# The state space quarters of a two-block transformer kernel: three elementwise products and a difference placed on GpSimd beside VectorE's scans

## The chip, the cores and the metric

One core of a Trainium2 chip runs the whole program. The metric is the device time of one execution in microseconds (us). All data are float32.

## The reference, cut to what matters

Two blocks run one behind the other on x of shape 1 x 256 x 1024. The first has attention, a pooling mixer and two grouped mixtures of experts; the second a mixer of two halves (mLSTM and a diagonal state space), a feed-forward layer, a gated linear mixer and another feed-forward layer. The change touches only the state space half:

```
ab_re, ab_im = mag * cos(a_im * dt), mag * sin(a_im * dt)
bu_re = einsum('blgp,gnp->blgn', ug, bb_re)
bu_im = einsum('blgp,gnp->blgn', ug, bb_im)
...
_, _, x_re, x_im = lax.associative_scan(_complex_affine_combine, (a_seq_re, a_seq_im, bu_re, bu_im), axis=1)
y = einsum('blgn,gpn->blgp', x_re, c_re) - einsum('blgn,gpn->blgp', x_im, c_im)
y = y + d_skip * ug
```

There are 32 groups of 64 states, 2048 complex states in all, over 256 steps.

## The kernel before, in words

The kernel is a list of stages. In each, TensorE, ScalarE, VectorE and GpSimd run a program of their own, and all wait for each other at the stage's end (`stage_done`, L231 to L237). Weights stream through a ring of six buffers, issued by SyncE. `mixer_ab` (L1877) is one such stage: `all_pe` (L1932), `all_act` (L2071), `all_dve` (L2112), and no program on GpSimd. The output projection behind it is the next stage (`project_out`, L1780, its matmuls at L1789), and the feed-forward layer follows.

The 2048 states are worked in four quarters of 512 (four columns of 128 partitions, 256 steps each), so an array of one quarter is 128 x 1024. The complex recurrence is made real: the input is turned back by the angle of the step, the two parts are scanned with the real decay `mag`, and the result is turned forward. `cosT` and `sinT` hold the tables. For quarter c:

- `states(c)` (TensorE, L1944) puts the real and imaginary inputs in PSUM and signals `bu_ready`.
- `turn_in` (VectorE, L2118, products at L2127): four products of a PSUM operand and a table, into z0, z1, t_re, t_im; the last signals `bu_taken`.
- `turned_in` (L2131): z0 += t_re (L2133), z1 -= t_im (L2134).
- `scans` (L2136): eight scans of 128 x 256, real and imaginary by turns (L2139, L2140), from z0 to t_re and z1 to t_im. The decay is one column repeated.
- `turn_out` (L2143): z0 = t_re cos (L2146), z1 = t_im cos (L2147), t_re *= sin (L2148), t_im *= -sin (L2149); the last signals `x_ready`.
- `outputs(c)` (TensorE, L1954, matmuls at L1960) waits for `x_ready` and signals `y_ready`; `take_y` (L2151, L2153) adds the skip term.

The tiles z0, z1 lie in the ring buffer's scratch, t_re in `xn`, t_im in `gates`, the tables in `arena`: all in SBUF. The trace uses these names.

The mLSTM half is interleaved by hand. VectorE's order (L2265 to L2312): quarter 0; four convolutions (L2158, L2161), each waiting for its projection tile, which ScalarE takes from PSUM (L2074); `take_y(0)`; quarter 1; `forget`; `take_y(1)`; `log_forget`; quarter 2 with `sums` (L2183, waits for TensorE's running sums, L2038 to L2040) between its scans and `turn_out`; `running_max`; `take_y(2)`; quarter 3 with the attention-like pieces between its parts: `floor`, `weigh(h)` (L2202, one SBUF and one PSUM operand) and `finish(h)` (L2210 to L2215: small ops on 128 x 2, two of them with two SBUF operands, then two of 128 x 128 from PSUM); then the norms and the gates.

TensorE's order (L1994 to L2069): projections to the state space with `states(0)` and `states(1)` among them; `outputs(0)`; the q, k, v blocks and `states(2)`; the gate products (48 matmuls of 8 columns, L2025); `outputs(1)`; the Z projections (L1941, 64 matmuls, `states(3)` among them); the running sums; `outputs(2)`; scores and mixes by head; `outputs(3)`.

Of the kernel before, what the change touches and what calls it, by code (L numbers as in the profile page):

```python
# [13 lines left out]
ALU = mybir.AluOpType  # L14
# [139 lines left out]
def build_program(nc, A, out):  # L154

    with ExitStack() as ctx:
# [3 lines left out]
        def sem(name):  # L160
            return ctx.enter_context(nc.semaphore(name))
# [20 lines left out]
        col_at, n = {}, 0  # L182
# [38 lines left out]
        chain = {}  # L221
# [87 lines left out]
        cosT, sinT = take(S_PAIRS, S), take(S_PAIRS, S)  # L309
# [254 lines left out]
        x_ready, h_act, h_dve = sem("x_ready"), sem("h_act"), sem("h_dve")  # L564
# [1312 lines left out]
        def mixer_ab():  # L1877
# [6 lines left out]
            for c in range(2):  # L1884
# [11 lines left out]
            t1, t2, t3, b_tok, a_tok, m_tok = (take(TT, 4) for _ in range(6))  # L1896
# [5 lines left out]
            a_rows, m_rows = scratch[:, 5632:5888], scratch[:, 5888:6144]  # L1902
            z = scratch[:, 6144:8192].rearrange("p (a q s) -> p a q s", a=2, q=4)
# [9 lines left out]
            den = small[:, 36:52].rearrange("p (h t b) -> p h t b", h=4, t=2)  # L1913
            var_ready, sd_ready = head_norm_signals
            exp_ready, ln_ready = log_sigmoid_signals
            (tile_ready, tile_taken, spread_ready, conv_ready, conv_done, abs_ready, lf_ready, b_ready, a_ready, aT_ready,
             m_ready, mT_ready, em_ready, qk_ready, ex_ready, w_ready, num_ready, num_taken, hn_ready, hnT_ready) = (
                sem("ab_" + n) for n in (
                    "tile_ready", "tile_taken", "spread_ready", "conv_ready", "conv_done", "abs_ready", "lf_ready", "b_ready",
                    "a_ready", "aT_ready", "m_ready", "mT_ready", "em_ready", "qk_ready", "ex_ready", "w_ready", "num_ready",  # L1920
                    "num_taken", "hn_ready", "hnT_ready"))
            bu_ready, bu_taken, x_ready, y_ready, y_taken, g_done, glu_ready, sig_ready = (
                sem("s5_" + n) for n in ("bu_ready", "bu_taken", "x_ready", "y_ready", "y_taken", "gelu_done", "glu_ready",
                                         "glu_sig_ready"))
            US, XM, QKV, VT, GATES, Z = 0, 4, 8, 20, 22, 23
            QK, LG, NUM, GLU, Y = (4, 0), (5, 1), (6, 2), (3, 7, 0, 1), 7

# [4 lines left out]
            def all_pe(pe):  # L1932
# [19 lines left out]
                    ins.then_inc(bu_ready, 1)  # L1952

                def outputs(c):  # L1954
                    pe.wait_ge(x_ready, c + 1)
                    if c:
                        pe.wait_ge(y_taken, c)
                    for i, (n, part) in enumerate(((0, z[:, 0]), (1, z[:, 1]), (1, t_re), (0, t_im))):
                        for q in range(4):
                            ins = pe.matmul(ps[32 * q:32 * q + 32, Y, 0:S], CT[:, n, c, 32 * q:32 * q + 32], part[:, q, :],  # L1960
                                            start=(i == 0), stop=(i == 3))
                    ins.then_inc(y_ready, 1)
# [71 lines left out]
                release(pe)  # L2034

                pe.wait_ge(tile_taken, Z + 4)
                pe.wait_ge(lf_ready, 1)
                pe.matmul(ps[:, 4, 0:4], const("upto"), t1[:, 0, :], start=True, stop=True)  # L2038
                pe.matmul(ps[:, 4, 4:8], ones, t1[:, 0, :], start=True, stop=False)
                pe.matmul(ps[:, 4, 4:8], const("upto"), t1[:, 1, :], start=False, stop=True).then_inc(b_ready, 1)  # L2040
                pe.wait_ge(a_ready, 1)
# [4 lines left out]
                pe.wait_ge(m_ready, 1)  # L2046
# [5 lines left out]
                for h in range(4):  # L2052
                    if h < 3:
                        scores(h + 1)
                    if h == 0:
                        pe.wait_ge(em_ready, 1)
                    mix(h)
                outputs(3)
                w = ring.take(pe, ("glu",))
# [11 lines left out]
            def all_act(act):  # L2071
# [16 lines left out]
                act.wait_ge(abs_ready, 1)  # L2088
# [5 lines left out]
                for h in range(4):  # L2094
                    act.wait_ge(qk_ready, h + 1)
                    if h >= 2:
                        act.wait_ge(w_ready, h - 1)
                    lg = ps[:, LG[h % 2], :]
                    act.activation(expd[:, h % 2, 0:S], lg[:, 0:S], ACT.Exp, bias=a_tok[:, 0, h:h + 1])
                    act.activation(expd[:, h % 2, S:W], lg[:, S:W], ACT.Exp, bias=a_tok[:, 1, h:h + 1]).then_inc(ex_ready, 1)  # L2100
                    if h == 0:
                        act.wait_ge(em_ready, 1)
# [9 lines left out]
            def all_dve(dve):  # L2112
                v = chain["dve"]
# [15 lines left out]
                        ins.then_inc(bu_taken, 1)  # L2129

                def turned_in(c):  # L2131
                    dve.wait_ge(bu_taken, c + 1)
                    dve.tensor_tensor(z[:, 0], z[:, 0], t_re, ALU.add)  # L2133
                    v(dve.tensor_tensor(z[:, 1], z[:, 1], t_im, ALU.subtract))  # L2134

                def scans(c, pairs):  # L2136
                    for q in pairs:
                        decay = pc[:, 0, 4 * c + q:4 * c + q + 1].to_broadcast([P, S])
                        dve.tensor_tensor_scan(t_re[:, q, :], decay, z[:, 0, q, :], 0.0, ALU.mult, ALU.add)  # L2139
                        ins = dve.tensor_tensor_scan(t_im[:, q, :], decay, z[:, 1, q, :], 0.0, ALU.mult, ALU.add)  # L2140
                    v(ins)

                def turn_out(c):  # L2143

                    co, si = rotation(c)
                    dve.tensor_tensor(z[:, 0], t_re, co, ALU.mult)  # L2146
                    v(dve.tensor_tensor(z[:, 1], t_im, co, ALU.mult))  # L2147
                    dve.tensor_tensor(t_re, t_re, si, ALU.mult)  # L2148
                    dve.scalar_tensor_tensor(out=t_im, in0=t_im, scalar=-1.0, in1=si, op0=ALU.mult, op1=ALU.mult).then_inc(x_ready, 1)  # L2149

                def take_y(c):  # L2151
# [18 lines left out]
                def forget():  # L2170
                    dve.wait_ge(tile_taken, GATES + 1)
                    v(dve.tensor_tensor(pre, pre, b_if.unsqueeze(1).to_broadcast([P, TT, 8]), ALU.add))
                    v(dve.tensor_scalar(t2, f, -1.0, None, ALU.mult))
                    dve.tensor_tensor(t2, f, t2, ALU.min).then_inc(abs_ready, 1)
                    v(dve.tensor_scalar(t1, f, 0.0, None, ALU.min))

                def log_forget():
                    dve.wait_ge(ln_ready, 2)
                    dve.tensor_tensor(t1, t1, t2, ALU.subtract).then_inc(lf_ready, 1)

                def sums():
                    dve.wait_ge(b_ready, 1)
                    v(dve.tensor_copy(b_tok, ps[:, 4, 0:8].rearrange("p (t h) -> p t h", t=TT)))  # L2183
                    dve.tensor_tensor(a_tok, pre[:, :, 0:4], b_tok, ALU.subtract).then_inc(a_ready, 1)

                def running_max():
                    dve.wait_ge(aT_ready, 1)
                    v(dve.tensor_copy(a_rows[0:4, :], ps[0:4, 5, 0:S]))
                    v(dve.tensor_tensor_scan(m_rows[0:4, :], ones[0:4, 0:1].to_broadcast([4, S]), a_rows[0:4, :], 0.0,
                                             ALU.mult, ALU.max))  # L2190
                    dve.tensor_scalar(m_rows[0:4, :], m_rows[0:4, :], -1.0, None, ALU.mult).then_inc(m_ready, 1)

                def floor():
                    dve.wait_ge(mT_ready, 1)
                    dve.tensor_tensor(t1, b_tok, ps[:, 6, 0:2 * P].rearrange("p (t h) -> p t h", t=TT)[:, :, 0:4],
                                      ALU.subtract).then_inc(em_ready, 1)

                def weigh(h):
                    dve.wait_ge(ex_ready, h + 1)
# [65 lines left out]
                for i in range(4):  # L2265
                    turn_in(0, i)
                turned_in(0)
                scans(0, range(4))
                turn_out(0)
                for n in range(4):  # L2270
                    convolve(n)
# [1 line left out]
                for i in range(4):  # L2273
                    turn_in(1, i)
                turned_in(1)
                scans(1, range(4))
                turn_out(1)
                forget()
                take_y(1)
# [1 line left out]
                for i in range(4):  # L2281
                    turn_in(2, i)
                turned_in(2)
                scans(2, range(4))
                sums()
                turn_out(2)
                running_max()
# [4 lines left out]
                        floor()  # L2292
                turned_in(3)
                weigh(0)
                scans(3, range(2))
                weigh(1)
                finish(0)
                scans(3, range(2, 4))
                weigh(2)
                finish(1)  # L2300
                turn_out(3)
# [9 lines left out]
                mlstm_out()  # L2311
                glu_out(3)  # L2312

            stage(all_pe, all_act, all_dve)
            scratch_used = 4 * len(programs["pe"])
            stream.append(lambda sp: sp.wait_ge(stage_done, scratch_used))
            project_out("ab_out", mixT, 0, col("norm_g_2", 16, 8))
# [371 lines left out]
```

## Time and profile before

| | |
|---|---|
| median of 3 runs | 2192.69 us (2184.86 to 2197.79) |
| profiled execution, its own time | 2188.47 us |
| its span, first to last instruction | 2186.4 us |
| busy, TensorE / VectorE / ScalarE / GpSimd | 1731.5 / 501.8 / 218.1 / 97.9 us |
| mean granted TensorE clock | 0.881 of full speed |
| the `mixer_ab` stage's state space part | 1345 to 1454 us of the span |

The profiler calls the engines PE (matmul), PEld (weight load), DVE (VectorE), ACT (ScalarE), POOL (GpSimd) and SP (SyncE). A timeline row gives the start, the duration, the engine and line, the operation, its tiles as output<-inputs, their shapes and the number of instructions merged in the row; in brackets the idle time before it and what ended it. Consecutive VectorE instructions overlap a little in the records, so the distance from start to start is what one costs. Columns of the tables by stretch are explained at their first group below.

### The profile page before, as it was taken

How to read it: one execution, taken by the hardware profiler on the slowest of the kernel's cores; microseconds unless marked ns; L12 is line 12 of the kernel's file. 1: busy time of each engine (PE TensorE's matmuls, PEld its weight loads, DVE VectorE, ACT ScalarE, POOL GpSimd, SP SyncE). 2: the span in 40 equal slices, each digit the busy share in tenths (PEclk: the TensorE clock that was granted, in tenths of full speed). 3: DMA queues.
4: the chain of work that ended last, by engine and by line, in shares of the span. 5: the costliest groups of instructions: out<-in, count | busy, mean ns of one | idle time of the engine just before them, and what ended most of it. 6: DMA issues, size and time to landing. Idle time of an engine off the chain costs nothing. (4 is left out here: it accounts for less than half of the span.)

```text
span 2186.4 us, 22473 instructions
## 1 busy us (share of the span) xinstructions
PE 1731.5 (79%) x9018; PEld 1000.1 (46%) x9019; DVE 501.8 (23%) x1168; ACT 218.1 (10%) x510; POOL 97.9 (4%) x125
## 2 busy tenths in 40 slices
PE   5999978866666576776666657878999899889998
PEld 3755553322222253232222215646885486558853
DVE  1213362111101125411111016861000203420001
ACT  1001020000000020000000001321000212110000
POOL 1010010000000007500000000000000000000000
PEclk9999968978877867898787778889999899899999
DMA  9969249999999956799999994133335434124330
GB/s 363 385 234 406 93 181 402 421 422 422 422 422 422 409 233 250 322 406 421 422 422 422 422 408 158 39 140 122 142 107 210 164 116 154 39 87 154 116 135 19
DMA packets 122665, 581.10 MB, mean 266 GB/s; under 512 B 10820, under 2 KB 15272, under 8 KB 67160
## 3 DMA queue, kind: packets, MB, share of 16 engines
q1 hardware_dynamic: 120416, 573.90, 65.4%
q0 software_dynamic: 1104, 2.86, 0.4%
q10 hardware_dynamic: 1064, 3.17, 0.4%
q8 instruction: 60, 0.98, 0.2%
q14 instruction: 21, 0.17, 0.0%
HBM read 578.86 MB, written 1.05 MB: 265 GB/s over the span
## 5 line engine op out<-in xcount | busy, mean ns | idle before, releaser
L1306 PE MATMUL ps<-ring_buffer,arena 128*32 128x512 f32 x2048 | 309.6, 763 | 170.6 <-DMA ring_buffer<-in_exp_w 167.9
L1831 PE MATMUL ps<-hT,ring_buffer 128*128 128x256 f32 x1408 | 309.9, 382 | 4.1 <-issue 2.6
L1831 PEld LDWEIGHTS ps<-hT,ring_buffer 128*128 128x128 f32 x1408 | 268.7, 192 | 45.2 <-issue 6.3
L1306 PEld LDWEIGHTS ps<-ring_buffer,arena 128*32 128x32 f32 x2048 | 82.1, 135 | 384.8 <-issue 325.0
L1331 PE MATMUL ps<-ring_buffer,arena 128*32 128x512 f32 x1088 | 155.8, 725 | 100.3 <-DMA ring_buffer<-in_exp_w 89.3
L1839 PE MATMUL ps<-ring_buffer,arena 128*128 128x512 f32 x352 | 154.2, 595 | 3.0 <-DVE arena L1872 1.9
L1331 PEld LDWEIGHTS ps<-ring_buffer,arena 128*32 128x32 f32 x1088 | 41.0, 130 | 204.3 <-issue 191.6
L1496 DVE TENSOR_TENSOR arena<-arena,ps 128x512 f32<-128x512 f32 x18 | 19.2, 1065 | 411.6 <-PE ps L1306 411.6
L1839 PEld LDWEIGHTS ps<-ring_buffer,arena 128*128 128x128 f32 x352 | 65.9, 190 | 90.4 <-issue 87.8
L1276 PE MATMUL ps<-arena,xn 128*128 128x128 f32 x640 | 82.0, 289 | 12.9 <-DVE arena L1466 12.9
L1276 PEld LDWEIGHTS ps<-arena,xn 128*128 128x128 f32 x640 | 78.6, 203 | 28.1 <-issue 22.3
L2364 PE MATMUL ps<-hT,ring_buffer 128*128 128x256 f32 x384 | 87.1, 389 | 1.9 <-issue 1.0
L1872 DVE TENSOR_TENSOR arena<-arena,ps 128x256 f32<-128x256 f32 x44 | 18.5, 421 | 295.9 <-ACT arena L1866 295.9
L2364 PEld LDWEIGHTS ps<-hT,ring_buffer 128*128 128x128 f32 x384 | 74.4, 195 | 15.0 <-issue 3.5
L1419 ACT ACTIVATE arena<-ps,mod,gain 128x128 f32<-128x128 f32 x72 | 27.1, 457 | 419.0 <-PE ps L1276 419.0
L1789 PE MATMUL ps<-ring_buffer,hT 128*128 128x512 f32 x128 | 59.7, 627 | 3.3 <-DVEq L237 3.0
L715 PE MATMUL ps<-hT,ring_buffer 128*128 128x256 f32 x256 | 58.6, 391 | 3.2 <-ACTq L237 2.5
L1512 DVE TENSOR_TENSOR arena<-ps,gates 128x512 f32<-128x512 f32 x16 | 11.1, 692 | 211.8 <-PE ps L1331 211.8
L1345 PE MATMUL ps<-arena 128*128 128x512 f32 x128 | 59.3, 605 | 0.0
L499 PE MATMUL ps<-ring_buffer,arena 128*32 128x512 f32 x384 | 50.0, 642 | 9.2 <-DMA ring_buffer<-in_ada_w 8.3
L715 PEld LDWEIGHTS ps<-hT,ring_buffer 128*128 128x128 f32 x256 | 50.0, 197 | 13.0 <-issue 3.4
L1436 ACT ACTIVATE arena<-ps 128x512 f32<-128x512 f32 x18 | 10.8, 597 | 416.7 <-PE ps L1306 416.7
(501 smaller groups left out, 1565.5 us busy)
## 6 DMA issues: line engine op xcount, KB each, us to landing
ring_buffer<-in_exp_w SPq DMA_DIRECT2D x384, 1024.0 KB, 18.6
ring_buffer<-in_ffn_w SPq DMA_DIRECT2D x30, 2048.0 KB, 7.9
ring_buffer<-in_ada_w SPq DMA_DIRECT2D x24, 2048.0 KB, 12.6
ring_buffer<-in_c_w_in SPq DMA_DIRECT2D x8, 2048.0 KB, 7.8
ring_buffer<-in_attn_w_in SPq DMA_DIRECT2D x6, 2048.0 KB, 17.0
ring_buffer<-in_ab_w_in SPq DMA_DIRECT2D x3, 2048.0 KB, 19.8
ring_buffer<-in_ffn_w SPq DMA_DIRECT2D x6, 1024.0 KB, 7.8
ring_buffer<-in_attn_w_o SPq DMA_DIRECT2D x2, 2048.0 KB, 12.8
```

The lines of the kernel that those rows point to most:

```text
L499: pe.matmul(ps[g * WIDE:(g + 1) * WIDE, COND, :], spread_c[:, 2 * pair + k, row:row + WIDE], w[:, k, 512 * n:512 * (n + 1)], start=(first ...
L715: ins = pe.matmul(ps[:, n % BANKS, 0:S], w[:, k, j * P:(j + 1) * P], hT[:, k, :], start=(k == 0), stop=(k == KD - 1))
L1276: ins = pe.matmul(ps[:, BXA + k // 4, (k % 4) * P:(k % 4 + 1) * P], xn[:, t, k * P:(k + 1) * P], pick[:, t, :], start=(t == 0), stop=(t == ...
L1306: ins = pe.matmul(ps[c, bank, :], tokens[:, 4 * phase + k, c], halves[j][:, k, :], start=(phase == 0 and k == 0), stop=(phase == 1 and k = ...
L1331: ins = pe.matmul(ps[c, bank, :], tokens[:, 2 * phase + k, c], halves[j][:, k, half * 512:(half + 1) * 512], start=(phase == 0 and k == 0) ...
L1345: ins = pe.matmul(ps[:, 2 * half + t, :], weights[:, t, :], values[:, half * 512:(half + 1) * 512], start=opens, stop=False, skip_group_ch ...
L1419: return eng.activation(o, src, ACT.Identity, scale=G[:, k:k + 1], bias=H[:, k:k + 1])
L1496: dve.tensor_tensor(to.rearrange("c (h k p) -> c h p k", h=2, k=2), gated.rearrange("c (h p k) -> c h p k", h=2, k=2), ps[:, bank, :].rear ...
L1789: ins = pe.matmul(ps[:, 2 * c + t, :], fT[:, k, t * P:(t + 1) * P], w[:, k, :], start=(k == 0), stop=(k == KD - 1))
L1831: ins = pe.matmul(ps[:, f % 8, i * S:(i + 1) * S], w[:, k, j * P:(j + 1) * P], hT[:, k, :], start=(k == 0), stop=(k == KD - 1))
L1839: ins = pe.matmul(ps[:, 2 * half + t, :], aT[:, r + k, t * P:(t + 1) * P], w[:, k, 512 * half:512 * half + 512], start=(r + k == 0), stop= ...
L2364: ins = pe.matmul(ps[:, n % 8, 0:S], w[:, k, j * P:(j + 1) * P], hT[:, k, :], start=(k == 0), stop=(k == KD - 1))
```

## The change

GpSimd gets a program in this stage. It makes z1 -= t_im, z0 = t_re cos and t_re *= sin of each quarter; VectorE keeps the rest. The scans run real part first, all four, then the imaginary four: the imaginary ones wait for GpSimd's difference (`turned`), GpSimd's products wait for the real ones (`re_scanned`). `outputs(c)` waits until both engines have signalled `x_ready`. In quarter 3 the two groups of scans take the places of the two pairs. Five semaphores of the gate chain become one counter, `forget_step`, with the same order of signals.

```diff
                 def outputs(c):
-                    pe.wait_ge(x_ready, c + 1)
+                    pe.wait_ge(x_ready, 2 * c + 2)
...
                 def turned_in(c):
+
                     dve.wait_ge(bu_taken, c + 1)
-                    dve.tensor_tensor(z[:, 0], z[:, 0], t_re, ALU.add)
-                    v(dve.tensor_tensor(z[:, 1], z[:, 1], t_im, ALU.subtract))
-
-                def scans(c, pairs):
-                    for q in pairs:
+                    v(dve.tensor_tensor(z[:, 0], z[:, 0], t_re, ALU.add))
+
+                def scans(c, part):
+                    if part:
+                        dve.wait_ge(turned, c + 1)
+                    to = (t_re, t_im)[part]
+                    for q in range(4):
                         decay = pc[:, 0, 4 * c + q:4 * c + q + 1].to_broadcast([P, S])
-                        dve.tensor_tensor_scan(t_re[:, q, :], decay, z[:, 0, q, :], 0.0, ALU.mult, ALU.add)
-                        ins = dve.tensor_tensor_scan(t_im[:, q, :], decay, z[:, 1, q, :], 0.0, ALU.mult, ALU.add)
-                    v(ins)
+                        ins = dve.tensor_tensor_scan(to[:, q, :], decay, z[:, part, q, :], 0.0, ALU.mult, ALU.add)
+                    if part:
+                        v(ins)
+                    else:
+                        ins.then_inc(re_scanned, 1)
 
                 def turn_out(c):
 
                     co, si = rotation(c)
-                    dve.tensor_tensor(z[:, 0], t_re, co, ALU.mult)
                     v(dve.tensor_tensor(z[:, 1], t_im, co, ALU.mult))
-                    dve.tensor_tensor(t_re, t_re, si, ALU.mult)
                     dve.scalar_tensor_tensor(out=t_im, in0=t_im, scalar=-1.0, in1=si, op0=ALU.mult, op1=ALU.mult).then_inc(x_ready, 1)
...
                 weigh(0)
-                scans(3, range(2))
+                scans(3, 0)
                 weigh(1)
                 finish(0)
-                scans(3, range(2, 4))
+                scans(3, 1)
                 weigh(2)
...
-            stage(all_pe, all_act, all_dve)
+            def all_pool(pool):
+                v = chain["pool"]
+                for c in range(4):
+                    co, si = cosT[:, 4 * c:4 * c + 4, :], sinT[:, 4 * c:4 * c + 4, :]
+                    pool.wait_ge(bu_taken, c + 1)
+                    pool.tensor_tensor(z[:, 1], z[:, 1], t_im, ALU.subtract).then_inc(turned, 1)
+                    pool.wait_ge(re_scanned, c + 1)
+                    v(pool.tensor_tensor(z[:, 0], t_re, co, ALU.mult))
+                    pool.tensor_tensor(t_re, t_re, si, ALU.mult).then_inc(x_ready, 1)
+
+            stage(all_pe, all_act, all_dve, all_pool)
```

The calls `scans(c, range(4))` of quarters 0 to 2 become `scans(c, 0)` and `scans(c, 1)` in the same place.

## Rows read from the trace of the kernel before

**Rows 1.** The page, busy time, share of the span and instructions of each engine

```profile
PE 1731.5 (79%) x9018; PEld 1000.1 (46%) x9019; DVE 501.8 (23%) x1168; ACT 218.1 (10%) x510; POOL 97.9 (4%) x125
```

**Rows 2.** Busy time by stretch: start:end and us, busy us (instructions) by engine, PEclk, DMA, GB/s

```profile
1345.40:1454.50 109.10, 88.02 (x546) 70.33 (x546) 94.41 (x173) 27.74 (x51) 0.00 (x0) 0.89 0.11 39
```

**Rows 3.** Timeline of VectorE, quarter 0: start us, us, engine line op [idle before, releaser]

```profile
1350.10 1.23 DVE L2133 TENSOR_TENSOR ring_buffer<-ring_buffer,xn 128x1024 f32<-128x1024 f32 x1
1351.24 1.22 DVE L2134 TENSOR_TENSOR ring_buffer<-ring_buffer,gates 128x1024 f32<-128x1024 f32 x1
1352.49 0.69 DVE L2139 TENSOR_TENSOR_SCAN xn<-arena,ring_buffer 128x256 f32<-128x256 f32 x1
...
1357.29 1.23 DVE L2146 TENSOR_TENSOR ring_buffer<-xn,arena 128x1024 f32<-128x1024 f32 x1
...
1360.83 1.22 DVE L2149 SCALAR_TENSOR_TENSOR gates<-gates,arena 128x1024 f32<-128x1024 f32 x1
...
1368.58 0.41 DVE L2158 TENSOR_SCALAR arena<-arena,cols 128x256 f32<-128x256 f32 x1 [0.63 <-ACT arena L2074]
```

**Rows 4.** The same timeline, quarters 2 and 3

```profile
1396.09 1.23 DVE L2133 TENSOR_TENSOR ring_buffer<-ring_buffer,xn 128x1024 f32<-128x1024 f32 x1
...
1407.54 0.17 DVE L2183 COPY arena<-ps 128x8 f32<-128x8 f32 x1 [4.29 <-PE ps L2040]
...
1423.85 0.56 DVE L2202 TENSOR_TENSOR hT<-hT,ps 128x384 f32<-128x384 f32 x1
1424.32 0.68 DVE L2139 TENSOR_TENSOR_SCAN xn<-arena,ring_buffer 128x256 f32<-128x256 f32 x1
```

**Rows 5.** Timeline of TensorE in the same stage

```profile
1368.16 1.07 PE L1960 MATMUL ps<-ring_buffer,arena 128*32 128x256 f32 x16
...
1387.52 1.93 PE L1960 MATMUL ps<-ring_buffer,arena 128*32 128x256 f32 x16 [0.32 <-DVE gates L2149]
...
1390.75 7.17 PE L1941 MATMUL ps<-hT,ring_buffer 128*128 128x256 f32 x32
...
1412.62 1.93 PE L1960 MATMUL ps<-ring_buffer,arena 128*32 128x256 f32 x16 [4.28 <-DVE gates L2149]
```

**Rows 6.** Timeline of GpSimd, TENSOR_TENSORs of 128x1024

```profile
308.16 3.19 POOL L1588 TENSOR_TENSOR arena<-arena 128x1024 f32<-128x1024 f32 x1 [6.00 <-DMA arena<-in_pool_scale]
311.44 5.57 POOL L1592 TENSOR_TENSOR arena<-arena 128x1024 f32<-128x1024 f32 x2
...
868.98 2.34 POOL L463 TENSOR_TENSOR arena<-arena,hT 128x1024 f32<-128x1024 f32 x1
```

**Rows 7.** Timelines of VectorE (four rows) and of GpSimd (last row), beside each other

```profile
309.15 3.28 DVE L1131 TENSOR_TENSOR arena<-arena,consts 128x1024 f32<-128x1024 f32 x1
312.47 1.22 DVE L1132 TENSOR_REDUCE arena<-arena 128x32 f32<-128x1024 f32 x1
...
839.33 1.23 DVE L1131 TENSOR_TENSOR arena<-arena,consts 128x1024 f32<-128x1024 f32 x1
...
879.94 0.69 DVE L1514 TENSOR_TENSOR arena<-ps,gates 128x512 f32<-128x512 f32 x1 [1.40 <-PE ps L1331]
...
879.31 3.61 POOL L461 TENSOR_TENSOR hT<-arena 128x2048 f32<-128x2048 f32 x1
```

**Rows 8.** Timelines of VectorE (two rows) and of GpSimd (last row), 891 to 907 us

```profile
891.77 3.71 DVE L1466 TENSOR_TENSOR arena<-arena 128x256 f32<-128x256 f32 x1
...
906.97 0.43 DVE L1466 TENSOR_TENSOR arena<-arena 128x256 f32<-128x256 f32 x1
...
891.53 3.67 POOL L464 TENSOR_TENSOR hT<-arena 128x2048 f32<-128x2048 f32 x1
```

**Rows 9.** Busy time by stretch around TensorE's outputs(1) and outputs(2), columns as in rows 2

```profile
1387.50:1390.75 3.25, 3.23 (x32) 1.36 (x32) 0.56 (x4) 3.19 (x5) 0.00 (x0) 0.56 0.00 0
1390.75:1398.00 7.25, 7.25 (x40) 6.14 (x39) 7.00 (x8) 1.44 (x3) 0.00 (x0) 1.00 0.00 0
1412.60:1416.20 3.60, 3.58 (x33) 1.36 (x33) 1.25 (x3) 0.00 (x0) 0.00 (x0) 0.50 0.00 0
```

More of the change, by code:

```diff
@@ L1915, in mixer_ab @@
             exp_ready, ln_ready = log_sigmoid_signals
-            (tile_ready, tile_taken, spread_ready, conv_ready, conv_done, abs_ready, lf_ready, b_ready, a_ready, aT_ready,
-             m_ready, mT_ready, em_ready, qk_ready, ex_ready, w_ready, num_ready, num_taken, hn_ready, hnT_ready) = (
+            (tile_ready, tile_taken, spread_ready, conv_ready, conv_done, forget_step, b_ready, aT_ready, mT_ready, qk_ready,
+             ex_ready, w_ready, num_ready, num_taken, hn_ready, hnT_ready) = (
                 sem("ab_" + n) for n in (
-                    "tile_ready", "tile_taken", "spread_ready", "conv_ready", "conv_done", "abs_ready", "lf_ready", "b_ready",
-                    "a_ready", "aT_ready", "m_ready", "mT_ready", "em_ready", "qk_ready", "ex_ready", "w_ready", "num_ready",
+                    "tile_ready", "tile_taken", "spread_ready", "conv_ready", "conv_done", "forget_step", "b_ready",
+                    "aT_ready", "mT_ready", "qk_ready", "ex_ready", "w_ready", "num_ready",
                     "num_taken", "hn_ready", "hnT_ready"))
-            bu_ready, bu_taken, x_ready, y_ready, y_taken, g_done, glu_ready, sig_ready = (
-                sem("s5_" + n) for n in ("bu_ready", "bu_taken", "x_ready", "y_ready", "y_taken", "gelu_done", "glu_ready",
+            bu_ready, bu_taken, turned, re_scanned, x_ready, y_ready, y_taken, g_done, glu_ready, sig_ready = (
+                sem("s5_" + n) for n in ("bu_ready", "bu_taken", "turned", "re_scanned", "x_ready", "y_ready", "y_taken", "gelu_done", "glu_ready",
                                          "glu_sig_ready"))
+            ABS, LOG_FORGET, SUMS, MAX, FLOOR = 1, 2, 3, 4, 5
             US, XM, QKV, VT, GATES, Z = 0, 4, 8, 20, 22, 23
@@ L2036, in all_pe @@
                 pe.wait_ge(tile_taken, Z + 4)
-                pe.wait_ge(lf_ready, 1)
+                pe.wait_ge(forget_step, LOG_FORGET)
                 pe.matmul(ps[:, 4, 0:4], const("upto"), t1[:, 0, :], start=True, stop=True)
@@ L2040, in all_pe @@
                 pe.matmul(ps[:, 4, 4:8], const("upto"), t1[:, 1, :], start=False, stop=True).then_inc(b_ready, 1)
-                pe.wait_ge(a_ready, 1)
+                pe.wait_ge(forget_step, SUMS)
                 for t in range(TT):
@@ L2045, in all_pe @@
                 outputs(2)
-                pe.wait_ge(m_ready, 1)
+                pe.wait_ge(forget_step, MAX)
                 for t in range(TT):
@@ L2055, in all_pe @@
                     if h == 0:
-                        pe.wait_ge(em_ready, 1)
+                        pe.wait_ge(forget_step, FLOOR)
                     mix(h)
@@ L2087, in all_act @@
                 take_tile(GATES, pre, bank(GATES)[:, 0:16].rearrange("p (t n) -> p t n", t=TT))
-                act.wait_ge(abs_ready, 1)
+                act.wait_ge(forget_step, ABS)
                 act.activation(t3, t2, ACT.Exp).then_inc(exp_ready, 1)
@@ L2101, in all_act @@
                     if h == 0:
-                        act.wait_ge(em_ready, 1)
+                        act.wait_ge(forget_step, FLOOR)
                         act.activation(m_tok, t1, ACT.Exp, scale=-1.0).then_inc(exp_ready, 1)
@@ L2173, in forget @@
                     v(dve.tensor_scalar(t2, f, -1.0, None, ALU.mult))
-                    dve.tensor_tensor(t2, f, t2, ALU.min).then_inc(abs_ready, 1)
+                    dve.tensor_tensor(t2, f, t2, ALU.min).then_inc(forget_step, 1)
                     v(dve.tensor_scalar(t1, f, 0.0, None, ALU.min))
@@ L2178, in log_forget @@
                     dve.wait_ge(ln_ready, 2)
-                    dve.tensor_tensor(t1, t1, t2, ALU.subtract).then_inc(lf_ready, 1)
+                    dve.tensor_tensor(t1, t1, t2, ALU.subtract).then_inc(forget_step, 1)
                 def sums():
@@ L2183, in sums @@
                     v(dve.tensor_copy(b_tok, ps[:, 4, 0:8].rearrange("p (t h) -> p t h", t=TT)))
-                    dve.tensor_tensor(a_tok, pre[:, :, 0:4], b_tok, ALU.subtract).then_inc(a_ready, 1)
+                    dve.tensor_tensor(a_tok, pre[:, :, 0:4], b_tok, ALU.subtract).then_inc(forget_step, 1)
                 def running_max():
@@ L2190, in running_max @@
                                              ALU.mult, ALU.max))
-                    dve.tensor_scalar(m_rows[0:4, :], m_rows[0:4, :], -1.0, None, ALU.mult).then_inc(m_ready, 1)
+                    dve.tensor_scalar(m_rows[0:4, :], m_rows[0:4, :], -1.0, None, ALU.mult).then_inc(forget_step, 1)
                 def floor():
@@ L2195, in floor @@
                     dve.tensor_tensor(t1, b_tok, ps[:, 6, 0:2 * P].rearrange("p (t h) -> p t h", t=TT)[:, :, 0:4],
-                                      ALU.subtract).then_inc(em_ready, 1)
+                                      ALU.subtract).then_inc(forget_step, 1)
                 def weigh(h):
@@ L2267, in all_dve @@
                 turned_in(0)
-                scans(0, range(4))
+                scans(0, 0)
+                scans(0, 1)
                 turn_out(0)
@@ L2275, in all_dve @@
                 turned_in(1)
-                scans(1, range(4))
+                scans(1, 0)
+                scans(1, 1)
                 turn_out(1)
@@ L2283, in all_dve @@
                 turned_in(2)
-                scans(2, range(4))
+                scans(2, 0)
+                scans(2, 1)
                 sums()
```

## Prediction

> **What bounds the kernel now.** I read the busy shares first: TensorE 79% of the span, VectorE 23%, GpSimd 4% [rows 1]. Over the whole kernel VectorE is no bottleneck, and GpSimd is almost free. The share is an average, though, so next come the stretches. From 1345.4 to 1454.5 us, where the mixer's state space and mLSTM halves run interleaved, VectorE is busy 94.4 of 109.1 us and GpSimd 0 [rows 2]. The reader is to see that this is a VectorE stage inside a TensorE and DMA kernel; whatever VectorE loses or gains here moves everything behind it, because the output projection waits for its end.
>
> Then VectorE's own timeline of one quarter [rows 3]. T0 is the start of the sum after the four products from PSUM (1350.10). Sum and difference take until 1352.49, eight scans until 1357.29 (4.80), four products until 1362.05. So T0 to the signal x_ready is 11.95 us, and an op of 128x1024 costs 1.14 us from start to start.
>
> Last, what ends VectorE's idle time in the stage, as that decides how much of a shift gets through. Quarter 0: 0.63 us in front of the fourth convolution, for a projection tile [rows 3]. Quarter 1: only TensorE's outputs, which themselves start at x_ready, so that wait moves with it. Quarter 2: 4.29 us for TensorE's running sums (L2040), which follow outputs(1) and the Z projections [rows 4, 5]. Quarter 3: no wait between T0 and x_ready. TensorE in turn waits for x_ready by only 0.32 us in quarter 1 and by 4.28 us in quarter 2 [rows 5].
>
> **The change, part by part.**
> Removed from VectorE per quarter: the difference (L2134) and two products (L2146, L2148), 3 x 1.14 = 3.42 us; 13.7 us over four quarters. The reordering of the eight scans costs nothing: the same eight instructions. The merged semaphores (one counter in place of five) carry the same waits and cost nothing; POOL's queue is empty in this stage, so nothing is queued behind its new waits.
>
> Added on GpSimd per quarter: three TENSOR_TENSORs of 128x1024 with two full SBUF operands. The nearest rows are 2.34 us for that size with VectorE quiet, and 3.19 and 5.57/2 = 2.79 with VectorE busy [rows 6]. So 7.0 us per quarter, against 3.42 on VectorE. Only overlap can make this pay.
>
> Do they overlap? This is the heart of the case. While GpSimd ran its 128x1024 product at 308.16, VectorE's L1131 (two SBUF inputs) took 3.28 us; the same line alone takes 1.23 [rows 7]. So it stood still for 2.05 us. The TENSOR_REDUCE right behind it (one input) took its usual 1.22 beside the next GpSimd op, and a VectorE op with one PSUM and one SBUF input took its usual 0.69 in the middle of a GpSimd op of 3.61. Likewise a 128x256 TENSOR_TENSOR that takes 0.43 alone took 3.71 beside a GpSimd op of 3.67, a loss of 3.28, or 0.9 of the GpSimd op [rows 8]. Two-input SBUF work of the two engines does not overlap; it takes turns, whole instruction by whole instruction. The Trainium skill says so as a rule ("SBUF — State Buffer", Who interferes with whom): a VectorE instruction with two SBUF inputs contends with a GpSimd instruction that reads SBUF, as an exclusive lock. By that rule the scans, which read the decay and z from SBUF, are locked out too; no row here has a scan beside a GpSimd op.
>
> The price of one GpSimd op to VectorE is then 0.9 x 2.34 = 2.1 us (ends: 2.05 from L1131, 2.34 if all of it is lost). For a scan the two ends are 0 (it behaves as the one-input reduction) and 2.1 (as the two-input op). A scan has two SBUF inputs as L1131 has, so I take 2.1. All the VectorE work between T0 and x_ready, except the mLSTM pieces of quarter 3, is of this kind.
>
> Quarter 0: GpSimd's difference waits for the sum, then holds off the first scan; the two products come between the imaginary scans. 3 x 2.1 - 3.42 = +2.9 us at x_ready. TensorE's outputs(0) starts at 1368.16 [rows 5], long after 1365, so that costs nothing there; the convolutions behind x_ready absorb the 0.63 wait, so +2.3 on.
> Quarter 1: +2.9 again, with nothing to absorb it, as TensorE's outputs start at x_ready: +5.2.
> Quarter 2: before, the scans end 7.2 us after T0 (1396.09; 2.39 + 4.80, as in quarter 0) and sums() starts at 11.45, released by TensorE [rows 4]. After: 7.2 - 1.14 + 6.3 = 12.3, so sums() is late by 0.9, not by 2.9, and the two products behind it no longer stand on VectorE (-2.28): -1.4. Total +3.8. What is late next is the scans, not TensorE.
> Quarter 3: weigh(0) and weigh(1) read PSUM and one SBUF tile, 0.56 us long, about 0.47 from start to start [rows 4], and run beside GpSimd's difference and first product. The second product holds off the small two-input ops of finish(0). 6.3 - 2 x 0.47 - 3.42 = +1.9. Total +5.7. Behind x_ready(3) VectorE is the bound to the end of the stage, and its short waits there are for engines that wait for it, so all of this arrives; the feed-forward behind it is TensorE's and only moves.
>
> The profiled execution has span 2186.4 and time 2188.47; the sum gives 2194.2. It lies 4.2 us under the median of the runs shown (2192.69, of 2184.86 to 2197.79), so on the median: 2198.4, +0.26%. With 2.34 per GpSimd op it would be +8.5 (2201.2); with 2.05 some +5.3.
>
> **The rivals.**
> *The scans are not held off.* For it: no row shows a scan so, and one of the two inputs is a single repeated value. Then VectorE waits for GpSimd only in its own two products and the small ops. Quarter 0 gains 1.4 at x_ready, but the fourth convolution still waits for its projection tile, so nothing is left. Quarter 1 can gain 0.3, for TensorE's gate products end 0.32 us before outputs(1) [rows 5]. Quarter 2 loses the two products, -2.3. In quarter 3 finish(0) still waits (+3.7 against -3.4). Sum -2.3: 2190.4. If nothing at all collided, quarter 3 gave its 3.4 too: -6.0, 2186.7. Even this is less than 0.5% (11 us): the gain is capped by the convolution's tile and by TensorE's running sums, whatever GpSimd does.
> *Slower by over 0.5%: TensorE's clock.* In quarter 1 TensorE now idles some 3 us between its gate products and outputs(1), where it idled 0.32. The granted clock was 0.56 during outputs(1), and 1.00 in the Z projections behind them [rows 9]; these are the two levels, 1.2 and 2.4 GHz. Should the low level last through the first 32 Z matmuls (7.17 us at 1.00, so 14.3 at 0.50), sums() comes 7.2 late instead of 0.9: +12.0, 2204.7. It passes 0.5% once some 28 of the 32 run low. Against it: outputs(1) runs low before too, and the clock is at 1.00 for the stretch right behind it; outputs(2) shows that a wait of 4.28 us gives no more than the same low level, 0.50 [rows 5, 9].
>
> **How the numbers follow.** Forecast (all two-input work takes turns): 0.70. Scans free, or nothing collides: 0.17. Clock: 0.13. A measurement of this kernel can tell about 0.5% from no change; three runs differ by 0.6% among themselves, so each case spreads by some 4 us. Slower by over 0.5%: the clock case nearly whole (0.11) and the upper end of the forecast (0.07), 0.18. Faster by over 0.5%: only the free case with a low run, 0.05. Within: 0.77. The range takes in the free case at 2186.7 with little spread below it, and the forecast's upper end 2201 plus spread, with the clock case's centre: 2185 to 2206.
>
> **What would show it.** VectorE's sum of the real parts still at 1.22; the first real scan of quarters 0 to 2 some 2.8 us long instead of 0.69, and two imaginary scans likewise, each ending as a GpSimd op ends. T0 to x_ready 14.9 us in quarters 0 and 1. VectorE's waits for the tile (0.63) and the running sums (4.29) gone. GpSimd busy 28 to 36 us more. The stage's end near 1460. In quarter 3 an op of finish(0) with 128x2 elements that lasts about 2 us. The forecast's mechanism is wrong if the scans beside GpSimd keep 0.67; its size is wrong if the GpSimd products differ from 2.3 us once the waits are taken out, or if the Z projections show a clock under 1.00.

## The result and the profile after

The changed kernel takes 2190.70 us (median of 12 runs, 2182.14 to 2196.59). The kernel before, timed beside it, takes 2180.27 (12 runs, 2176.36 to 2197.79, among them the three shown at first, which lay high). The ratio is 1.0045, 95% interval 1.0026 to 1.0065; timed again it was 1.0039 (1.0019 to 1.0059). So the change makes the kernel slower by about 9 us, 0.4%, where I forecast 5.7 us, 0.26%.

The page of the profiled execution after, against [rows 1]:

```profile
span 2189.1 us, 22473 instructions
PE 1723.3 (79%) x9018; PEld 999.5 (46%) x9019; DVE 511.3 (23%) x1156; ACT 217.9 (10%) x510; POOL 132.0 (6%) x137
```

VectorE has 12 instructions fewer and is busy 9.5 us more. That is the result in one line: three ops a quarter left it, and waiting inside its instructions came in their place. GpSimd's 34.1 us are new.

The stage as one stretch, from the first of quarter 0's four products to its last VectorE instruction, columns as in [rows 2]:

```profile
1335.70:1450.60 114.90, 90.60 (x546) 71.55 (x546) 103.89 (x161) 27.73 (x51) 33.95 (x12) 0.87 0.11 37
```

Timeline of VectorE after, quarter 0 (as [rows 3]), then pieces of quarters 2 and 3 (as [rows 4]):

```profile
1340.38 1.22 DVE L2135 TENSOR_TENSOR ring_buffer<-ring_buffer,xn 128x1024 f32<-128x1024 f32 x1
1341.64 4.47 DVE L2143 TENSOR_TENSOR_SCAN xn<-arena,ring_buffer 128x256 f32<-128x256 f32 x4
1346.03 6.63 DVE L2143 TENSOR_TENSOR_SCAN gates<-arena,ring_buffer 128x256 f32<-128x256 f32 x4
1352.70 1.22 DVE L2152 TENSOR_TENSOR ring_buffer<-gates,arena 128x1024 f32<-128x1024 f32 x1
1353.95 1.23 DVE L2153 SCALAR_TENSOR_TENSOR gates<-gates,arena 128x1024 f32<-128x1024 f32 x1
...
1391.79 1.23 DVE L2135 TENSOR_TENSOR ring_buffer<-ring_buffer,xn 128x1024 f32<-128x1024 f32 x1
...
1397.44 6.62 DVE L2143 TENSOR_TENSOR_SCAN gates<-arena,ring_buffer 128x256 f32<-128x256 f32 x4
1404.10 0.17 DVE L2187 COPY arena<-ps 128x8 f32<-128x8 f32 x1
...
1417.47 4.00 DVE L2143 TENSOR_TENSOR_SCAN xn<-arena,ring_buffer 128x256 f32<-128x256 f32 x4
...
1422.03 1.90 DVE L2215 SCALAR_TENSOR_TENSOR small<-small 128x2 f32<-128x2 f32 x1
```

The reader is to see that VectorE is never idle in these pieces and still slow. T0 is again the start of a quarter's first sum. Four scans take 2.4 us when nothing disturbs them (eight take 4.80 in the kernel before, from 1352.49 to 1357.29 in [rows 3]); here the real ones take 4.47 and the imaginary ones 6.63. The wait is inside the instruction, so no table of waits lists it. In quarter 2 the wait of 4.29 us in front of the copy at 1404.10 is gone: it comes straight behind the scans, 12.31 us after T0. In quarter 3 an op on 128x2 elements takes 1.90 us.

Timeline of GpSimd after, quarters 0 and 3, beside it:

```profile
1340.51 3.31 POOL L2326 TENSOR_TENSOR ring_buffer<-ring_buffer,gates 128x1024 f32<-128x1024 f32 x1 [383.12 <-DVE gates L2128]
1346.20 2.65 POOL L2328 TENSOR_TENSOR ring_buffer<-xn,arena 128x1024 f32<-128x1024 f32 x1 [2.38 <-DVE xn L2143]
1348.92 2.61 POOL L2329 TENSOR_TENSOR xn<-xn,arena 128x1024 f32<-128x1024 f32 x1
...
1421.56 2.35 POOL L2328 TENSOR_TENSOR ring_buffer<-xn,arena 128x1024 f32<-128x1024 f32 x1 [2.38 <-DVE xn L2143]
1423.98 2.34 POOL L2329 TENSOR_TENSOR xn<-xn,arena 128x1024 f32<-128x1024 f32 x1
```

The difference (1340.51) is issued while VectorE's sum still runs and lasts 3.31 us, 1.0 more than the 2.34 of such an op with nothing in its way; the real scans behind the sum are held until it ends. The product that starts beside a scan (1346.20) takes 0.3 us longer than the one that starts beside an op with one SBUF and one PSUM input (1421.56): GpSimd waits in its turn as well. The op at 1422.03 ends at 1423.93, as the product from 1421.56 ends.

Two lengths carry the rest of this text. The stage: from VectorE's first sum to the end of its last gate product, 104.37 us before, 110.22 after. And the heads stage of the second mixer, 400 us later and untouched by the change, from its first matmul to the first one behind its heads (L2473 to L2597 in the kernel before): 34.5 us before, 41.7 after.

### The profile page after: what moved, and what is told of

Its sections match the earlier page's. It is cut to its first block and busy times, and to the rows that moved or that the text cites. A ratio compares the mean times of both kernels' runs of the same rounds, so it can differ in the third digit from the quotient of the medians.

```text
span 2189.1 us, 22473 instructions
## 1 busy us (share of the span) xinstructions
PE 1723.3 (79%) x9018; PEld 999.5 (46%) x9019; DVE 511.3 (23%) x1156; ACT 217.9 (10%) x510; POOL 132.0 (6%) x137
## 5 line engine op out<-in xcount | busy, mean ns | idle before, releaser
L1306 PE MATMUL ps<-ring_buffer,arena 128*32 128x512 f32 x2048 | 302.6, 748 | 177.2 <-DMA ring_buffer<-in_exp_w 174.8
L1331 PE MATMUL ps<-ring_buffer,arena 128*32 128x512 f32 x1088 | 153.1, 715 | 102.1 <-DMA ring_buffer<-in_exp_w 92.7
L499 PE MATMUL ps<-ring_buffer,arena 128*32 128x512 f32 x384 | 49.2, 633 | 8.8 <-DMA ring_buffer<-in_ada_w 7.9
```

Of the source, the lines that this page charges most:

```text
L499: pe.matmul(ps[g * WIDE:(g + 1) * WIDE, COND, :], spread_c[:, 2 * pair + k, row:row + WIDE], w[:, k, 512 * n:512 * (n + 1)], start=(first ...
L1306: ins = pe.matmul(ps[c, bank, :], tokens[:, 4 * phase + k, c], halves[j][:, k, :], start=(phase == 0 and k == 0), stop=(phase == 1 and k = ...
L1331: ins = pe.matmul(ps[c, bank, :], tokens[:, 2 * phase + k, c], halves[j][:, k, half * 512:(half + 1) * 512], start=(phase == 0 and k == 0) ...
```

## The experiments

All stage lengths are read from each run's own timeline of VectorE.

**Order only.** The scans keep the new order, everything is back on VectorE.

```diff
...
-            stage(all_pe, all_act, all_dve, all_pool)
+            stage(all_pe, all_act, all_dve)
```

> The changed kernel with its difference and products back on VectorE and no program on GpSimd; what is left of the change is the order of the scans (real, then imaginary) and the merged counter. Measure: from the first sum of quarter 0 to the stage's last VectorE instruction, 104.4 us in the kernel before and 110.2 in the changed one. Turn-taking theory: order costs nothing, so 104.4 within 0.4, T0 to x_ready 11.95 us per quarter, time as the kernel before. Rival (the new order of the scans or the counter costs the time): well over 105.

Stage 104.30 us, time 2178.72, ratio 0.9995 (0.9974 to 1.0016). The order and the merged counter cost nothing that can be seen.

**Difference only.** GpSimd keeps the subtraction; its two products go back to VectorE.

> Only the imaginary difference on GpSimd, both products back on VectorE. Turn-taking theory: the first real scan is held for some 2.1 us, 1.14 is saved; quarter 0 +1.0 at x_ready of which 0.6 goes into the wait for the projection tile, quarter 1 +1.0, quarter 2 nothing (the scans end 8.2 us after T0, ahead of TensorE's running sums at 11.45), quarter 3 +0.5: 106.3 us from first sum to stage end. Rival (scans run free beside GpSimd): 103.0 to 103.3.

Timeline of VectorE, quarter 0:

```profile
1345.61 1.23 DVE L2135 TENSOR_TENSOR ring_buffer<-ring_buffer,xn 128x1024 f32<-128x1024 f32 x1
1346.87 4.46 DVE L2143 TENSOR_TENSOR_SCAN xn<-arena,ring_buffer 128x256 f32<-128x256 f32 x4
```

The first real scan is held as in the changed kernel: 4.46 against 2.43 for four free ones (below), 2.03 us. Stage 107.2, not 106.3: the direction is the theory's, and it was 0.9 short (quarter 2 gave 0.4 where I had nothing, quarter 3 0.9 for 0.5). The time was out of proportion, though: ratio 1.0057 (1.0035 to 1.0079), 12 us, for 2.8 in the stage. The heads stage took 46.1.

**The decay in PSUM.** The same change, but a scan reads its decay from PSUM.

```diff
-                        decay = pc[:, 0, 4 * c + q:4 * c + q + 1].to_broadcast([P, S])
+                        decay = ps[:, Y, S + 4 * c + q:S + 4 * c + q + 1].to_broadcast([P, S])
...
+                dve.tensor_copy(ps[:, Y, S:S + S_PAIRS], pc[:, 0, :])
```

> The changed kernel, with the scans' decay column read from PSUM (one copy of 128x16 at the stage's start), so that a scan has one SBUF input in place of two; all else equal. Turn-taking by two SBUF inputs: no scan is held, eight scans take 4.7 to 4.8 us, GpSimd still takes turns with VectorE's sum, its last two products and the small ops of quarter 3; T0 to x_ready some 10.5 us in quarters 0 and 1, first sum to stage end 102 to 103 us, time 0.3 to 0.4% under the changed kernel's. Rival (GpSimd's busy time slows VectorE's SBUF writes or any op): scans stay held, 110 us.

Timelines of VectorE (four rows) and GpSimd (three rows), quarter 0:

```profile
1341.93 2.43 DVE L2143 TENSOR_TENSOR_SCAN xn<-ps,ring_buffer 128x256 f32<-128x256 f32 x4
1344.28 2.40 DVE L2143 TENSOR_TENSOR_SCAN gates<-ps,ring_buffer 128x256 f32<-128x256 f32 x4
1346.72 1.23 DVE L2152 TENSOR_TENSOR ring_buffer<-gates,arena 128x1024 f32<-128x1024 f32 x1
1347.98 3.25 DVE L2153 SCALAR_TENSOR_TENSOR gates<-gates,arena 128x1024 f32<-128x1024 f32 x1
...
1340.79 3.31 POOL L2327 TENSOR_TENSOR ring_buffer<-ring_buffer,gates 128x1024 f32<-128x1024 f32 x1 [379.87 <-DVE gates L2128]
1344.44 2.36 POOL L2329 TENSOR_TENSOR ring_buffer<-xn,arena 128x1024 f32<-128x1024 f32 x1 [0.34 <-DVE xn L2143]
1346.88 3.26 POOL L2330 TENSOR_TENSOR xn<-xn,arena 128x1024 f32<-128x1024 f32 x1
```

This settles the mechanism for the scans. Beside GpSimd's difference the real ones take 2.43 in place of 4.47, and beside its first product the imaginary ones take 2.40 in place of 6.63, when one operand comes from PSUM. It is no clash over one tile either: the difference does not read `arena`, where the decay lay, and the scans still read `ring_buffer`, as it does. What is left of the collision is where both engines still have two SBUF inputs: GpSimd's last product waits for L2152, then L2153 waits 2.03 us for it. T0 to x_ready 10.56 us, as expected. Stage 100.21, better than my 102 to 103. The Trainium skill's rule ("SBUF — State Buffer", Who interferes with whom), that a VectorE instruction with two SBUF inputs contends with a GpSimd one that reads SBUF, held here for scans too: 6.63 us against 2.40. The time is 0.36% under the changed kernel's, as expected. Against the kernel before it gained nothing, though the stage is 4.2 us shorter: ratio 1.0009 (0.9992 to 1.0027), with a heads stage of 46.1.

**GpSimd only writes.** Three memsets a quarter at the places of its three ops, which compute nothing; all arithmetic is on VectorE.

> All arithmetic on VectorE in the new order as in the order-only kernel; GpSimd runs three memsets of 128x704 per quarter at the points where the changed kernel has its three ops, so it writes SBUF beside the scans and reads nothing. Turn-taking between two-input reads and GpSimd's reads: no scan is held, 104.4 within 0.5 from first sum to stage end. Rival (any GpSimd access to SBUF holds VectorE): each memset adds its own length, some 1 us or more each, so 108 or more.

Timelines of VectorE and of GpSimd (last two rows), quarter 0:

```profile
1346.77 2.44 DVE L2143 TENSOR_TENSOR_SCAN xn<-arena,ring_buffer 128x256 f32<-128x256 f32 x4
1349.12 2.41 DVE L2143 TENSOR_TENSOR_SCAN gates<-arena,ring_buffer 128x256 f32<-128x256 f32 x4
...
1349.32 0.69 POOL L2329 MEMSET arena<- 128x704 f32 x1 [4.17 <-DVE xn L2143]
1350.06 0.68 POOL L2330 MEMSET arena<- 128x704 f32 x1
```

Two memsets run beside the imaginary scans and cost them nothing. Stage 104.38 us; had each of the twelve held VectorE for its own 0.69, it would be some 8 us more. It takes GpSimd's reads, not its mere presence or its writes. Whether a GpSimd op with a single SBUF input holds VectorE as well was not tried: every one that did so here is a TENSOR_TENSOR.

**The running sums later.** The kernel before with one swap; nothing on GpSimd.

```diff
                 scans(2, range(4))
-                sums()
                 turn_out(2)
+                sums()
```

> The kernel before with one edit: in quarter 2 sums() behind turn_out(). VectorE makes its four products in the 4.3 us in which it waited for TensorE's running sums, so outputs(2) starts some 4 us sooner: 100.4 us from first sum to stage end, 0.18% less time. Nothing on GpSimd. Rival (running_max, whose input turn_out() used to hide, now stands in the open): 102 or more. Heads stage: 34.5 if GpSimd's arithmetic decides about it; if it is chance, either.

Timeline of VectorE, quarter 2:

```profile
1391.44 1.22 DVE L2149 SCALAR_TENSOR_TENSOR gates<-gates,arena 128x1024 f32<-128x1024 f32 x1
1392.57 0.16 DVE L2183 COPY arena<-ps 128x8 f32<-128x8 f32 x1
1392.76 0.17 DVE L2184 TENSOR_TENSOR arena<-small,arena 128x8 f32<-128x8 f32 x1
1393.40 0.41 DVE L2188 COPY ring_buffer<-ps 4x256 f32<-4x256 f32 x1 [0.47 <-PE ps L2043]
```

The four products fill the old wait of 4.29 us; 0.47 is what running_max now waits. Stage 99.48 us, 4.9 less than before and 0.9 less than expected. The time fell by less and cannot be told from no change, ratio 0.9988 (0.9972 to 1.0004): the heads stage took 41.7 us in the profile, with no arithmetic on GpSimd.

**A version that beats both.** The decay in PSUM, only the difference and the first product on GpSimd, and the running sums later. The diff leaves out the decay and the swap, which are as above.

```diff
                     v(dve.tensor_tensor(z[:, 1], t_im, co, ALU.mult))
-                    ... t_im = -t_im * si ... .then_inc(x_ready, 1)
+                    ... t_im = -t_im * si ...
+                    dve.wait_ge(x_ready, 2 * c + 1)
+                    dve.tensor_tensor(t_re, t_re, si, ALU.mult).then_inc(x_ready, 1)
...
-                    v(pool.tensor_tensor(z[:, 0], t_re, co, ALU.mult))
-                    pool.tensor_tensor(t_re, t_re, si, ALU.mult).then_inc(x_ready, 1)
+                    pool.tensor_tensor(z[:, 0], t_re, co, ALU.mult).then_inc(x_ready, 1)
```

> A version meant to beat both kernels: decay column in PSUM, GpSimd makes only the difference and the first product (z0), VectorE takes t_re *= sin back, and in quarter 2 sums() stands behind turn_out() in place of ahead of it. If GpSimd's ops cost VectorE nothing where VectorE reads one SBUF input, T0 to x_ready is 9.4 to 9.7 us in quarters 0 and 1, and quarter 2 gains some 4 us by the reordering: 99 us from first sum to stage end against 104.4 before and 110.2 in the changed kernel, so 5 us under the kernel before. Rival (the time outside the stage depends on whether GpSimd works in it: the heads stage of the second mixer took 34.5 us in the profiles of the kernels with nothing or memsets on GpSimd, 41.7 to 46.1 in the three with arithmetic there): stage 99, heads stage over 41, total within 0.2% of the kernel before.

Stage 97.48 us (expected 99), T0 to x_ready 9.67 in quarter 0 (1349.20 to 1358.87), time 2174.76, ratio 0.9977 (0.9961 to 0.9993). It is 6.9 us shorter in the stage than the kernel before and 12.7 than the changed one. Of the 6.9, the swap alone gives 4.9; GpSimd's help gives 2.0. In the time the two kernels cannot be told apart (2174.80 with the swap alone, measured beside it): only the combined one is clear of the kernel before. Heads stage 34.5, with arithmetic on GpSimd. Together with the swap alone (41.7, none) this refutes the rival that GpSimd's work by itself decides how long the heads stage takes.

**Repeats.**

> The changed kernel once more, for the spread of its parts. First sum to stage end 110.2 within 0.3. Heads stage: over 41 us if it is the change that slows it, 34.5 in some profiles if it is chance.

> The kernel before once more. First sum to stage end 104.4 within 0.3. Heads stage: 34.5 if it is the change that slows it, over 41 in some profiles if it is chance.

> The changed kernel, timed again. In the stage it is 5.85 us longer, 0.27%; its first timing gave a ratio of 1.0045 (1.0026 to 1.0065). If the rest is chance (the heads stage at a low or a high TensorE clock, drawn anew in each execution), the ratio falls nearer to 1.0027; if something outside the stage is systematic, it stays near 1.0045.

> The difference-only kernel, timed again. In the stage it is 2.8 us longer than the kernel before, 0.13%; its first timing gave 1.0057 (1.0035 to 1.0079) from 6 runs. Chance: the ratio falls to 1.000 to 1.003. Systematic (GpSimd arithmetic in the stage slows something outside it): it stays over 1.004, and the heads stage is long in this profile too.

The stage repeats to 0.1 us: 110.22 and 110.24; 104.47; 107.22. The heads stage: changed kernel 41.7, 36.9, 36.9; before 34.5, 34.5; difference only 46.1, 46.1. The second timings give 1.0039 and 1.0055 (1.0038 to 1.0072). So what lies outside the stage is no chance of one measurement: both times came back, and so did the heads stage of two of the three kernels.

**Delay alone.** The kernel before with memsets on VectorE that nobody needs, ahead of the last gate (4, or 8 and a quarter).

```diff
...
                 mlstm_out()
+                for _ in range(4):
+                    v(dve.memset(spare[:, 0:640], 0.0))
                 glu_out(3)
```

> The kernel before with four memsets of a dead region (128x640) on VectorE ahead of the stage's last gate: 2.8 us of delay and nothing else, so the stage ends as late as in the difference-only kernel (107.2 us after its first sum). If the heads stage's clock hangs on when this stage ends, and not on what GpSimd does in it, the heads stage takes some 46 us here too and the time is over 0.4% longer than before; if it hangs on GpSimd's work, the heads stage stays at 34.6 and the time is 0.13% longer.

> The same with eight and a quarter memsets, some 5.9 us, so the stage ends as late as in the changed kernel (110.2). By the timing of the stage's end: the output projection takes 28.2 us in place of 30.0 and the heads stage 37 to 42, as in the changed kernel, time 1.003 to 1.005. By GpSimd's work: 30.0 and 34.6, time 1.0027.

Stages 107.65 and 111.05 us (0.4 and 0.8 later than aimed at), heads stage 34.5 in both, output projection 30.4 and 30.3: neither went as the timing theory had it. Yet the ratios of time are 1.0040 (1.0018 to 1.0063) and 1.0058 (1.0030 to 1.0086), more than the 3.3 and 6.7 us of their stages (0.15 and 0.31%), though both intervals reach down to about these values. A late stage end alone, at these two values, does not make the profiled heads stage longer; if something else lengthens the timed runs, their profiles do not show it.

What happens in the heads stage itself can be read. Its matmuls as one stretch, in the kernel before, the changed one and the one with the difference only (columns as in [rows 2]), and last 35 us within the latter:

```profile
1862.61:1891.29 28.68, 27.37 (x176) 19.65 (x176) 14.03 (x47) 6.77 (x36) 0.00 (x0) 0.88 0.16 61
1856.82:1892.65 35.83, 34.57 (x176) 24.76 (x176) 14.13 (x47) 6.76 (x36) 0.00 (x0) 0.67 0.13 48
1861.42:1901.64 40.22, 38.97 (x176) 27.46 (x176) 14.14 (x47) 6.78 (x36) 0.00 (x0) 0.57 0.12 45
1866.42:1901.42 35.00, 35.00 (x148) 24.40 (x148) 11.48 (x38) 6.03 (x34) 0.00 (x0) 0.51 0.00 1
```

The same 176 matmuls, and TensorE idle for 1.3 us in each; what differs is the granted clock. Shorter stretches, first the kernel before, then the changed one, then the kernel with the swap alone:

```profile
1871.00:1880.00 9.00, 8.98 (x52) 6.22 (x52) 4.44 (x15) 1.80 (x10) 0.00 (x0) 0.78 0.00 0
1880.00:1889.00 9.00, 8.96 (x66) 6.39 (x66) 5.08 (x19) 2.70 (x15) 0.00 (x0) 1.00 0.01 2
```

```profile
1865.00:1874.00 9.00, 9.00 (x38) 6.16 (x37) 2.80 (x9) 0.98 (x6) 0.00 (x0) 0.50 0.00 0
1874.00:1883.00 9.00, 9.00 (x38) 6.42 (x37) 3.61 (x12) 1.72 (x10) 0.00 (x0) 0.50 0.00 0
```

```profile
1849.00:1858.00 9.00, 9.00 (x38) 6.31 (x37) 2.61 (x9) 1.44 (x9) 0.00 (x0) 0.50 0.00 0
1858.00:1867.00 9.00, 9.00 (x38) 6.24 (x38) 3.61 (x12) 1.25 (x9) 0.00 (x0) 0.50 0.00 0
```

TensorE is busy all the time in each; at a granted clock of 0.50, the lower of the two levels (1.2 of 2.4 GHz), it gets through 76 matmuls in 18 us, where the kernel before, at 0.78 and 1.00, gets through 118. The clock is at the low level for a while in every kernel, the one before included (0.56 from 1867.61 to 1872.61); what differs is how long it stays there.

All parts side by side, in us, from the profiles. The last column but one runs from the first sum to the kernel's last instruction. It leaves out what lies ahead of that sum, which no edit changes but for the copy of 128x16 and which still took between 1334.7 and 1350.1 us in these profiles, so their total spans say little:

| kernel | stage | output projection | heads | first sum to the end | ratio of time |
|---|---|---|---|---|---|
| before, and its repeat | 104.4, 104.5 | 29.9, 29.9 | 34.5, 34.5 | 836.3, 836.4 | 1 |
| changed, and its repeats | 110.2 (three times) | 28.2 (three times) | 41.7, 36.9, 36.9 | 848.8, 843.2, 843.1 | 1.0045, 1.0039 |
| order only | 104.3 | 29.9 | 34.5 | 836.3 | 0.9995 |
| GpSimd writes only | 104.4 | 29.9 | 34.5 | 836.4 | |
| difference only, and its repeat | 107.2, 107.2 | 29.9, 29.9 | 46.1, 46.1 | 849.5, 849.6 | 1.0057, 1.0055 |
| decay in PSUM | 100.2 | 29.9 | 46.1 | 842.7 | 1.0009 |
| running sums later | 99.5 | 28.2 | 41.7 | 838.1 | 0.9988 |
| beats both | 97.5 | 29.9 | 34.5 | 829.6 | 0.9977 |
| delay of 3 us | 107.7 | 30.4 | 34.5 | 839.9 | 1.0040 |
| delay of 6 us | 111.1 | 30.3 | 34.5 | 843.2 | 1.0058 |

For the changed kernel, the difference alone and the version that beats both, the column "first sum to the end" agrees with the ratio of time. With the decay in PSUM and with the swap it shows some 4 us more than the timing, with the delays 5 to 6 us less: one profile need not stand for all executions.

## Why the prediction was right, point by point

- **The mechanism** was right: two-input SBUF work takes turns, scans included. I took the upper end of a range from 0 to 2.1 us for the hold of a scan; it measured 2.04 for the difference (4.47 - 2.43) and 2.11 for each product ((6.63 - 2.40) / 2). The stage ended at 1450.6 and not near 1460 because its first sum came 9.7 us sooner in this profile; counted from there the two agree.
- **Quarter 0 and 1.** T0 to x_ready 14.80 us (1340.38 to 1355.18) against 11.95: +2.85, forecast +2.9. Behind the convolutions +2.26 was left (+2.3); take_y(1) comes +5.42 after the first sum (+5.2); 0.3 of that is TensorE, whose outputs(1) took 3.6 us at a granted clock of 0.50 where they took 3.3 at 0.56.
- **Quarter 2.** sums() at 12.31 us after T0, forecast 12.3; take_y(2) +4.0 in all, forecast +3.8. The scans took the place of TensorE's running sums as what is late, as said.
- **Quarter 3** had two errors that cancel. At x_ready the total is +5.08 and not +5.7: the holds sum to 4.6 us (1.58 in the real scans, 1.74 in the small op, 1.31 in the imaginary ones), where I had 5.4. And I let "all of this arrive" behind it; in fact VectorE's wait for outputs(3) grew from 0.77 to 1.57 us. At the stage's end +5.85, forecast +5.7. That these agree so well is luck. TensorE's outputs(3) start 2.1 us behind x_ready in both kernels; the longer wait is their clock, 0.50 for 0.67, first before, then after:

```profile
1439.66:1442.50 2.84, 2.83 (x33) 1.23 (x32) 1.97 (x9) 0.00 (x0) 0.00 (x0) 0.67 0.01 3
1435.01:1438.66 3.65, 3.65 (x33) 1.38 (x32) 1.97 (x9) 0.00 (x0) 0.00 (x0) 0.50 0.00 0
```

With the 0.3 us of outputs(1), some 1.1 us of the 5.85 are TensorE's clock, and the turn-taking itself gave 4.7 where I had 5.7.

- **The clock rival** named a real effect and got its place and size wrong. The wait ahead of outputs(1) grew to 1.67 us and not to 3, for TensorE itself came 3.7 us later, 1.5 of it because the 24 matmuls behind outputs(0) took 6.92 us where they had taken 5.42 (granted clock 0.77 for 1.00). The Z projections lost 0.65 us, at a clock of 0.91, which I had named as a sign that my size was off:

Timeline of TensorE after (as [rows 5]):

```profile
1382.90 1.93 PE L1961 MATMUL ps<-ring_buffer,arena 128*32 128x256 f32 x16 [1.67 <-DVE gates L2153]
1384.60 1.08 PE L1961 MATMUL ps<-xn,arena 128*32 128x256 f32 x8
1385.46 1.08 PE L1961 MATMUL ps<-gates,arena 128*32 128x256 f32 x8
1386.47 7.82 PE L1942 MATMUL ps<-hT,ring_buffer 128*128 128x256 f32 x32
```

7.82 against 7.17, and the slack of quarter 2 hid it. The larger loss of clock stood 470 us later, in the heads stage; no run shows that the one leads to the other.

- **The step that failed** is the sentence that the feed-forward and all behind it "only moves". Of the three profiles of the changed kernel, two add up so: +5.85 in the stage, -1.7 in the output projection (its first 10 us ran at a clock of 1.00 where they had 0.83), +2.4 in the heads stage, some +0.4 in between, 6.9 in all (0.32%); the third has +7.1 in the heads stage and 1.4 behind it, 12.5 in all (0.57%). The measured 0.39 and 0.45% lie between. So my 0.26% was right for the stage and lacked 3 to 4 us for the rest of the kernel.
- **The base.** I put the sum on the median of three runs, 2192.69; twelve gave 2180.27. The forecast of 2198.4 is 7.7 us over the measured 2190.7: the base was 12.4 too high, the change 4.7 too small against the two medians (5.7 for 10.4), and the two errors partly cancel, which is luck too. The range of 2185 to 2206, moved down by 12.4, would hold 2190.7 as well.

What stays open: what sets the clock that the heads stage is granted. Neither GpSimd's work nor a late end of the stage explains all rows of the table.

## What to carry to other kernels

In these runs, arithmetic moved from VectorE to GpSimd overlapped with VectorE's scans and with `weigh(h)` where one of their two operands came from PSUM, and memsets overlapped with all that they stood beside; beside VectorE instructions with two SBUF inputs each GpSimd op of 2.35 us cost VectorE 2.1. So first look for a row where both engines work at once, and for one of the very operation: one SBUF input is not always enough. In the kernel before, a TENSOR_SCALAR with one SBUF input and constants took 2.48 us beside a GpSimd TENSOR_TENSOR and ended with it, where it takes 0.16 alone (VectorE, VectorE, GpSimd):

```profile
884.15 2.48 DVE L1489 TENSOR_SCALAR arena<-arena 128x4 f32<-128x4 f32 x1
...
905.86 0.16 DVE L1489 TENSOR_SCALAR arena<-arena 128x4 f32<-128x4 f32 x1
...
883.00 3.61 POOL L462 TENSOR_TENSOR arena<-arena 128x2048 f32<-128x2048 f32 x1
```

Putting one operand in PSUM, here a single column of decays, bought the overlap back. And before an engine is unloaded, see which waits cap the gain: here a swap of two calls into an existing wait was worth 4.9 us of the stage, GpSimd's help on top of it 2.0.

## What was not expected

A stage that the change does not touch, 400 us behind it, took 34.5, 36.9, 41.7 or 46.1 us, the same value again for the same kernel in most repeats, with TensorE idle for 1.3 us at most before its last matmul and the granted clock between 0.50 and 1.00. In the difference-only kernel it ran 35 us without a gap at a mean clock of 0.51. An edit early in a kernel can so come with 10 us elsewhere (difference only: 2.8 us in the stage, 13 from its first sum to the end, in both profiles); single stages have to be compared in the profile before a total of 0.5% is explained. The spread between executions of one and the same kernel goes with the clock as well: of the kernel before, one of 2169.22 us had a mean granted clock of 0.896, one of 2192.64 us 0.881.
